# Who subtracts for the weights' rests: VectorE in place of GpSimd, in a two-layer hybrid backbone kernel

## What is computed

```
per layer:
  h  = rmsnorm(x) * (1 + scale) + shift              (scale, shift from the conditioning vector)
  ym = sigmoid(h @ w_mo) * headnorm(mLSTM(h @ w_mq, h @ w_mk, h @ w_mv, gates))    4 heads, both directions
  ya = windowed attention(rope(h @ w_aq), rope(h @ w_ak), h @ w_av, sink)          8 heads on 2
  yr = silu(h @ w_rg) * headnorm(retention(h @ w_rq, h @ w_rk, h @ w_rv))          4 heads, both directions
  y  = (sigmoid(h @ w_gm) * (ym @ w_br_m) + sigmoid(h @ w_ga) * (ya @ w_br_a)
        + sigmoid(h @ w_gr) * (yr @ w_br_r)) @ w_out
  x  = x + g1 * y
  x  = x + g2 * (silu(conv3(h2 @ up_a) + b) * (h2 @ up_b)) @ w_down                 inner width 2816
output: rmsnorm(x) of the latent tokens
```

## Time and profile before

| | |
|---|---|
| three executions | 3015.2, 3002.2, 3006.5 us (median 3006.5) |
| profiled execution | 3000.0 us, of which its span 2998.2 us |
| TensorE (PE) busy | 2847.7 us, 95% of the span |
| DVE busy | 1198.2 us, 40% |
| ACT busy | 994.3 us, 33% |
| POOL busy | 1169.4 us, 39% |
| mean granted TensorE clock | 0.98 of full speed |

### The profile page before, as it was taken

One profiled execution on the slowest core, in us unless ns is written; L12 is line 12 of the kernel. 1 busy time (PEld: TensorE's weight loads), 2 busy tenths in 40 slices (PEclk: granted clock), 3 DMA queues, 4 the chain that ended last, 5 costly groups with the idle time before them and its releaser, 6 DMA issues. The chain is left out here.

```text
span 2998.2 us, 48255 instructions
## 1 busy us (share of the span) xinstructions
PE 2847.7 (95%) x19520; PEld 2563.6 (86%) x19520; DVE 1198.2 (40%) x2765; ACT 994.3 (33%) x1696; POOL 1169.4 (39%) x1048
## 2 busy tenths in 40 slices
PE   7999999999999999999999989999999999799998
PEld 5899889998889997888888779988988889788776
DVE  4554536523332023333333635436523321243435
ACT  4332236533322124222222333325532332333332
POOL 2233321153443424434343434331163355465654
PEclk9999999999999999999999999999999999899999
DMA  5111210022222133111211322131023222322222
GB/s 228 57 57 64 78 64 22 16 88 85 85 71 85 57 144 152 64 64 57 71 71 57 119 93 71 50 113 43 22 102 128 85 85 86 126 84 99 85 99 105
DMA packets 39386, 249.82 MB, mean 83 GB/s; under 512 B 4480, under 2 KB 4864, under 8 KB 13568
## 3 DMA queue, kind: packets, MB, share of 16 engines
q1 hardware_dynamic: 36288, 236.25, 21.9%
q10 hardware_dynamic: 2880, 10.49, 0.9%
HBM read 236.23 MB, written 10.49 MB: 82 GB/s over the span
## 5 line engine op out<-in xcount | busy, mean ns | idle before, releaser
L2174 POOL TENSOR_TENSOR w_rest<-raw,w_head 128x512 fp32r<-128x512 f32 (+1 forms) x642 | 843.7, 1345 | 1018.8 <-ACT w_head L1246 984.8
L867 PE MATMUL psum_products<-w_head,h_head 128*128 128x256 f32 x2368 | 686.3, 290 | 3.3 <-POOL w_rest L2174 3.3
L867 PE MATMUL psum_products<-w_rest,h_head 128*128 128x256 f32 x2368 | 663.1, 280 | 0.0
L867 PE MATMUL psum_products<-w_head,h_rest 128*128 128x256 f32 x2368 | 662.7, 280 | 0.0
L867 PE MATMUL psum_products<-h_head,w_head 128*128 128x512 f32 (+3 forms) x1696 | 601.5, 355 | 12.7 <-POOL w_rest L2174 8.7
L867 PE MATMUL psum_products<-h_rest,w_head 128*128 128x512 f32 (+3 forms) x1696 | 596.6, 352 | 0.0
L867 PE MATMUL psum_products<-h_head,w_rest 128*128 128x512 f32 (+3 forms) x1696 | 596.0, 351 | 0.0
L867 PEld LDWEIGHTS psum_products<-w_head,h_head 128*128 128x128 f32 x2368 | 451.6, 191 | 7.2 <-POOL w_rest L2174 3.7
L867 PEld LDWEIGHTS psum_products<-w_rest,h_head 128*128 128x128 f32 x2368 | 451.4, 191 | 1.8 <-issue 0.5
L867 PEld LDWEIGHTS psum_products<-w_head,h_rest 128*128 128x128 f32 x2368 | 450.7, 190 | 0.0
L1246 ACT ACTIVATE w_head<-raw 128x2048 fp32r<-128x2048 f32 (+2 forms) x170 | 307.5, 1809 | 431.6 <-PE psum_products L867 381.0
(11 more groups left out here) (267 smaller groups left out, 4006.3 us busy)
## 6 DMA issues: line engine op xcount, KB each, us to landing
raw<-in_stream SPq DMA_DIRECT2D x184, 1024.0 KB, 4.8
raw<-in_stream SPq DMA_DIRECT2D x16, 512.0 KB, 3.3
mods_mid<-in_stream SPq DMA_DIRECT2D x8, 1024.0 KB, 9.7
residual<-stage ACTq DMA_DIRECT2D x16, 512.0 KB, 2.8
stage<-residual SPq DMA_DIRECT2D x14, 512.0 KB, 5.8
mods_b<-in_stream SPq DMA_DIRECT2D x5, 1024.0 KB, 24.3
mods_a<-in_stream SPq DMA_DIRECT2D x3, 1024.0 KB, 13.6
x_in<-in_x SPq DMA_DIRECT2D x4, 512.0 KB, 8.5
```

Source lines behind the costliest of these rows:

```text
L867: return nc.tensor.matmul(o, a, b, start=start, stop=stop)
L2174: G.tensor_tensor(wl[:, s["sp"] % 2, a:b], place_of(s)[:, a:b], wh[:, s["sp"] % 2, a:b].bitcast(F32), ALU.subtract).then_inc(*ev.mark("poo ...
```

## The change

DVE issues the subtractions in place of POOL, at the same steps of the list. DVE now waits for the head of the slot, and the release of `raw` is marked by DVE. Nothing else is changed; the instructions have the same shapes and types. Lines of the kernel behind line 1609 are nine higher afterwards (L1924 becomes L1933).

```
@@ the loop of DVE
             for i, st in walk("dve"):
                 kind, s = st["kind"], st["slot"]
                 l, hd, t = st.get("l"), st.get("hd"), st.get("t")
+                if kind == "split":
+                    n = s["kt"] * s["cols"]
+                    dve.wait_ge(*ev.at("head", s["n"]))
+                    for a in range(0, n, SLOT // 4):
+                        b = min(n, a + SLOT // 4)
+                        V.tensor_tensor(wl[:, s["sp"] % 2, a:b], place_of(s)[:, a:b],
+                                        wh[:, s["sp"] % 2, a:b].bitcast(F32), ALU.subtract).then_inc(
+                                            *ev.mark("dve", "rest", s["n"]))
+                    ev.now[("raw_free", s["n"])] = {"dve": ev.count["dve"]}
                 if kind == "region":
@@ the loop of POOL
-                if kind == "split":
-                    n = s["kt"] * s["cols"]
-                    pool.wait_ge(*ev.at("head", s["n"]))
-                    for a in range(0, n, SLOT // 4):
-                        b = min(n, a + SLOT // 4)
-                        G.tensor_tensor(wl[:, s["sp"] % 2, a:b], place_of(s)[:, a:b],
-                                        wh[:, s["sp"] % 2, a:b].bitcast(F32), ALU.subtract).then_inc(
-                                            *ev.mark("pool", "rest", s["n"]))
-                    ev.now[("raw_free", s["n"])] = {"pool": ev.count["pool"]}
-                elif kind == "enter":
+                if kind == "enter":
```

## The result

The changed kernel takes 3054.1 us (median of four executions, 3043.7 to 3057.5) against 3009.6 us before (median of four). The ratio is 1.0143, with a 95% interval of 1.0108 to 1.0179: slower by 1.4%, as forecast in direction (3040 us, range 2978 to 3076). Its profiled execution has a span of 3049.5 us, 51.3 more than that of before.

The account below looks back on a forecast made before the run. TensorE was taken as the bound, busy 2847.7 of 2998.2 us. Gains of 42 us and losses of 78 summed to +36 on the profiled 3000.0, so 3036, put at 3040 us for the median; range 2978 to 3076.

Parts of the forecast that it names:

- The price of the work: Moved subtractions: four take DVE 2.75 us in place of some 5.1 on POOL; 642 add about 440 us to DVE.
- The place in DVE's order decides: At splits, DVE waits for the head, then subtracts 2.75 us, pushing later work; free where DVE had waited anyway.
- Start: At the kernel's start, DVE's copies come behind the second slot's head, a push of 8.4 us; +5.5 us taken.
- mLSTM: Splits inside mLSTM, both layers: pushed DVE work delays TensorE, less shorter waits for `w_rest`; net +29.2 us.
- Attention: Six attention splits, both layers: DVE pushes of 3.0 to 4.5 us, +18.9; one 1.8 us wait goes; net +17.1.
- Retention: Retention, both layers: 15.6 us of waits for `r_s` vanish, loads -4.0, `w_rest` -2.6; net -22.2 us.
- w_out and norms: Output projection and norms: two waits for `w_rest` go, -3.3 us; push on the vectors' copies +1.8; net -1.5.
- MLP: Down slots: DVE's late additions make TensorE wait for banks, while `w_rest` waits go; net +9.2 and -1.2 us by layer.
- B: Rival, chance 0.12: TensorE's order has slack at the splits, so POOL waits go and nothing comes back; 2964 us.
- C: Rival, chance 0.2: losses are half of those read, 39 us, and gains stay; 3003 us, within error of no change.
- D: Rival, chance 0.14: pushes in mLSTM, attention, start and down projections reach TensorE in full; +80 us, 3086 us.
- E: Rival, chance 0.06: DVE's subtraction ends later than POOL's had, so projections wait for `rest`; some +10 us on the forecast.

Follow-up runs that it names:

- e2_mixers_pool: Changed kernel, but POOL subtracts for the 30 slots split inside mLSTM and attention, DVE for all others; 2979.0 us, ratio 0.9918 to the kernel before.
- e4_mixers_dve: Changed kernel, but DVE subtracts only for the slots inside mLSTM and attention, POOL for all others; 3063.5 us, ratio 1.0198 to the kernel before.
- e5_late: Changed kernel, but inside mLSTM's tiles and attention DVE subtracts one mixer step later; 2998.2 us, ratio 0.9974 to the kernel before.
- e1_wait_only: Kernel before, with only DVE's wait for each slot's head added; POOL still does all 642 subtractions; 3048.3 us, ratio 1.0146.
- e3_chosen: Changed kernel, but POOL keeps the 30 mixer slots and twelve more at the start, vectors and down projections; 2953.6 us, ratio 0.9835 to before.
- e8_pe_waits: Kernel with POOL keeping mixer and twelve more slots, plus TensorE waiting for the head at the 30 mixer splits; 3111.5 us, ratio 1.0359 to before.
- e6_half: Changed kernel, but DVE subtracts the first half of each slot and POOL the second; 3058.6 us, ratio 1.0183 to the kernel before.

## Why the prediction was right, and where it was not

- **What bounds the kernel**: right. What decided was in every run what TensorE waited for, not how full DVE was (49%).
- **The price of the work**: right, 694 ns for 687. Four in a row take 2.50 us and not 2.75, since each starts 0.6 us after the last: a mis-sized term, 0.25 us at each push. DVE's busy time is 1486 us, where 1640 less 60 of relieved contention was expected: the relief is 117 us.
- **The place in DVE's order decides**: right, and shown for the place as a whole. The loss goes when POOL keeps 30 slots (e2_mixers_pool), stays when only these 30 move (e4_mixers_dve), and goes with all the work on DVE but one step later (e5_late). How it divides into the wait and the work behind it is not shown: e1_wait_only adds hold-ups by POOL to the wait.
- **Start**: +5.5 forecast, +6.8 measured; the wait of 8.12 us is the push of 8.4.
- **mLSTM**: the totals are right (19.6 and 9.6 forecast, 19.8 and 10.4 measured), but by luck, since the reason given is not what happened. As idle time the first split costs 3.46 - 1.38 = 2.1 us and not 3.8, the second 2.7 and not 3.2. The stages' idle time grew by 12.4 and 4.0 us; the other 7.4 and 6.4 us are busy time at a lower clock, which the sum had no term for.
- **Attention**: too low, 17.1 forecast and 27.5 measured. The idle time grew by 10.5 us only. The new waits behind the six splits (2.1, 3.9 and 2.0 us in layer 0, 3.2, 3.4 and 2.7 in layer 1) are 17.2 us in all, near the 18.9 of the sum, but beside the one for `w_rest` other waits shrank that it had kept: in layer 0 two for `a_y` (1.2 and 1.3 us) are gone, in layer 1 one for `a_q_split` fell from 2.6 us to 1.4. The other 17.0 us are again longer busy time.
- **Retention**: -22.2 forecast, -18.2 measured. The waits for `r_s` went as forecast: POOL's from 13.3 us to none and DVE's from 2.9 to 1.0, 15.2 less for 15.6. The term of the loads was too high: the waits for `raw` in retention went from 4.05 us to 3.49, a gain of 0.6 and not of 4.0.
- **w_out and norms**: -1.5 forecast, +1.0 measured. The idle time went as forecast, by -1.9 us: TensorE waits 5.5 us for `vrow` before the MLP, but there a wait of 3.4 us for `xs` is gone as well as those for `w_rest`. What makes the stage of layer 0 longer is 3.2 us of busy time. In e2_mixers_pool the same wait of 5.5 us brought none: that stage is 0.9 us shorter than before.
- **MLP**: +9.2 forecast and +9.7 measured in layer 0; four waits of 1.21 us for 1.6, and one of 5.32 for 5.6. In layer 1 -5.9 for -1.2: TensorE waits at none of its four other down slots, which accounts for 1.6, and 3.1 us are shorter busy time.
- **The step that failed** is the sum itself, as one of idle time alone: it put TensorE's clock at nothing. The sum was +36 us; the idle time grew by 18, so it was twice too large, and the clock brought 33 more. By the prediction's own signs it was wrong on the side "if the granted clock drops behind them": it dropped. The two errors offset each other down to 15 us of the span, and that the total lies so near the forecast is luck; the direction is not.
- **Rivals.** B, that the slack holds, is refuted in mixers and down slots, but describes e3_chosen, in which only the hidden places are moved: 2954 us, where B said 2964. C, that the losses are half of what was read, misses the total (3003), but in idle time alone the result, +18 us, lies midway between C (-3) and the forecast (+36). D, that nothing is absorbed, misses with 3086: mLSTM lost 30 us in both layers and not 60. A late DVE can make the next head late, but not by much: in the first mLSTM head of layer 0 the second of ACT's heads starts 12.9 us behind the first (133.14 against 120.20), where it was 11.9 before. E, that projections come to wait for the rest, is one wait of 1.7 us.

## What to carry to other kernels

When work moves to an idle engine that executes in order, price the wait in front of it and what is queued behind, place by place, and not the engine's share of busy time: here the same 642 instructions made the kernel 1.4% slower, 0.3% faster with the ones in the mixers issued one step later, and 1.7% faster with 42 of 170 slots left where they were. The choice of engine can be made per place; what is late on the bound engine's path should stay on the engine that is free there. And an idle spell of TensorE can cost more than its length, through its clock: here 33 us beside 18 of idle time, and 50 beside 103. A forecast that adds up waits needs a term for it.

## What the runs showed of the hardware

- **TensorE's clock.** It has two levels (1.2 and 2.4 GHz), and the granted clock falls to the lower one behind some of the waits of TensorE: it was 0.50 behind one of 3.46 us (at 198.54 in the changed kernel) and 1.00 behind another of 3.46 us (at 125.21). With 111 us of waits for the head added in 30 places and nothing else, the same matmuls took 50.5 us longer and the mean clock fell from 0.984 to 0.964 (e8_pe_waits against e3_chosen). Between before and after it was 33 us on 18 us of idle time, so the extra cost is not in a fixed ratio to the wait; what sets it at a single wait stays open.
- **DVE and POOL together.** A subtraction of 128x512 takes 694 ns on DVE (the changed kernel) and 1348 on POOL (the kernel before) in the mean, and 1216 and 1772 when both have two at the same time (e6_half). Other instructions of DVE are held up too: in e1_wait_only one of 128x1, 0.15 us before, took 1.27 us beside POOL's subtractions.
